# Seven-product rounds of a gated feed-forward: a chunk loaded in halves, copies moved behind product copies, one plain chunk more

## The reference

```python
mod = c_act @ w_ada[l] + b_ada[l]          # 6 x 1024 columns; the second block has 3 x 1024 more
...
h2 = rmsnorm(x, g_ffn[l]) * (1.0 + sc2) + sh2
gate, up = jnp.split(h2 @ w_gu[l], 2, axis=-1)      # D_FF = 2816 columns each
x = x + ga2 * ((jax.nn.silu(gate) * up) @ w_down[l])
```

## Time and profile before

| what | value |
|---|---|
| median of the runs (lowest, highest) | 1082.65 us (1078.78, 1084.9) |
| the profiled execution | 1086.33 us |
| its span in the profile | 1084.3 us |
| PE busy with matmuls | 1030.2 us, 95% |
| DVE, POOL, ACT busy | 755.5, 513.4 and 503.8 us |

### The profile page before, as it was taken

How to read it: one execution, slowest core, us unless ns; L and a number is a source line. 1 busy time by engine, 2 the same in 40 slices (tenths; PEclk the granted TensorE clock), 3 DMA queues, 4 the chain that set the end, 5 groups by cost and what they waited for, 6 DMA issues and landing times.

```text
span 1084.3 us, 15812 instructions
## 1 busy us (share of the span) xinstructions
PE 1030.2 (95%) x5814; PEld 862.4 (80%) x5814; DVE 755.5 (70%) x1423; ACT 503.8 (46%) x773; POOL 513.4 (47%) x209
## 2 busy tenths in 40 slices
PE   6999999999996898899989999999999999999997
PEld 5787796678885898899978788888887777888886
DVE  5367997787767344445549884579999999977322
ACT  4244335882454444544473223253445788363142
POOL 0034353681368544455543334345873767634350
PEclk9999999999999999989999999999999999999999
DMA  9984231141222223222239892323323222322312
GB/s 326 349 270 128 75 105 39 40 157 40 78 78 76 77 87 109 77 77 78 78 104 297 281 297 72 114 78 118 114 89 106 78 78 78 117 79 78 116 39 77
DMA packets 127257, 128.98 MB, mean 119 GB/s; under 512 B 3553, under 2 KB 125281, under 8 KB 127201
## 3 DMA queue, kind: packets, MB, share of 16 engines
q1 hardware_dynamic: 125952, 127.38, 36.4%
q10 hardware_dynamic: 1248, 0.86, 0.3%
HBM read 126.13 MB, written 2.10 MB: 118 GB/s over the span
## 4 chain that ended last, share of the span: by engine, by line
PE 69%; issue 12%; POOL 9%; DVE 4%; ACT 3%; DMA 2%; SPq 1%; POOLq 0%; DVEq 0%; ACTq 0%
PE bank L817 15%; PE bank L819 14%; PE bank L818 14%; POOL w_a L750 2%; POOL w_lo L653 2%; PE bank L1164 2%; PE bank L1135 2%; POOL w_hi L750 2%; PE bank L1007 2%; POOL w_s L757 2%; PE bank L1447 1%; PE bank L1449 1%; PE bank L1448 1%; DVE ff_lo L2534 1%; DMA ada_stage<-in_w_ada 1%
## 5 line engine op out<-in xcount | busy, mean ns | idle before, releaser
L653 POOL TENSOR_TENSOR w_lo<-w_stage,w_hi 128x2048 fp32r<-128x2048 f32 x59 | 283.2, 4801 | 376.9 <-ACT w_hi L1520 376.9
L817 PE MATMUL bank<-act_hi,w_hi 128*128 128x512 f32 x544 | 216.6, 398 | 3.5 <-POOL w_lo L653 3.5
L819 PE MATMUL bank<-act_hi,w_lo 128*128 128x512 f32 x544 | 212.1, 390 | 0.0
L818 PE MATMUL bank<-act_lo,w_hi 128*128 128x512 f32 x544 | 212.0, 390 | 0.0
L1520 ACT ACTIVATE w_hi<-w_stage 128x2048 fp32r<-128x2048 f32 x60 | 114.8, 1914 | 145.5 <-PE bank L819 133.0
L2698 DVE SCALAR_TENSOR_TENSOR bank<-v_pad,vcol,bank 128x512 f32<-128x512 f32 x208 | 138.2, 748 | 0.0
L817 PEld LDWEIGHTS bank<-act_hi,w_hi 128*128 128x128 f32 x544 | 102.2, 188 | 30.8 <-POOL w_lo L653 5.5
L818 PEld LDWEIGHTS bank<-act_lo,w_hi 128*128 128x128 f32 x544 | 102.3, 188 | 21.9 <-issue 1.4
L819 PEld LDWEIGHTS bank<-act_hi,w_lo 128*128 128x128 f32 x544 | 102.1, 188 | 21.5
L817 PE MATMUL bank<-ff_hi,w_hi 128*128 128x512 f32 x176 | 72.0, 409 | 3.5 <-POOL w_lo L653 3.5
L750 POOL TENSOR_TENSOR w_a<-w_stage,w_a 128x1024 fp32r<-128x1024 f32 x18 | 43.6, 2445 | 61.4 <-ACT w_a L1794 61.4
(11 more groups left out here) (404 smaller groups left out, 2610.1 us busy)
## 6 DMA issues: line engine op xcount, KB each, us to landing
w_stage<-in_w_in SPq DMA_DIRECT2D x29, 1024.0 KB, 5.2
w_stage<-in_w_gu SPq DMA_DIRECT2D x22, 1024.0 KB, 5.1
ada_stage<-in_w_ada SPq DMA_DIRECT2D x20, 1024.0 KB, 11.4
w_stage<-in_w_out SPq DMA_DIRECT2D x12, 1024.0 KB, 5.2
late_stage<-in_mod_w SPq DMA_DIRECT2D x12, 1024.0 KB, 8.4
w_stage<-in_w_down SPq DMA_DIRECT2D x8, 1024.0 KB, 5.3
late_stage<-in_w_ada SPq DMA_DIRECT2D x4, 1024.0 KB, 10.9
w_stage<-in_pw_w SPq DMA_DIRECT2D x4, 1024.0 KB, 5.4
```

Of the source, the lines that this page charges most:

```text
L653: nc.gpsimd.tensor_tensor(w_lo[b][:], w_stage[b][:], w_hi[b][:].bitcast(F32), ALU.subtract).then_inc(s_lo, 1)
L817: pe.matmul(dst, wh, rhs_hi(k), start=(first and k == 0), stop=False)
L818: pe.matmul(dst, wh, rhs_lo(k), start=False, stop=False)
L819: mm = pe.matmul(dst, wl, rhs_hi(k), start=False, stop=(last and k == n_k - 1))
```

## The change

- `PLAIN` is 3: three pairs of chunks are plain and eight are rounds. So there is one pair of 96 matmuls with 512 columns more and one round of 168 with 256 columns less.
- In the rounds the up chunk is loaded in two halves with a semaphore for the low one (`s_half`): the low half as soon as it has been copied and `w_diff` made, ahead of the gate chunk in SP's queue; the high half where the whole chunk was loaded. `copy_up_low` and `w_diff` wait for the low half, `weight_sum(0, 0)` and `block_hi(w_a22)` for the high one.
- In the round on ACT, `copy_block(p2_half[1])` stands ahead of `copy_up_low`, and `low_silu(1)` ahead of the second `gate_hi`.
- Ahead of the rounds the sums `h_sum` are made by DVE, no longer by POOL, and at once after the first plain chunk; the parts of `t_1`, `t_3`, `t_2` come ahead of the weight blocks.
- In the last round product 5 comes after products 6 and 7, and the parts of `ff` and of the first down chunk are made earlier.
- The late modulation columns: 6, 4, 6 between the steps for 5, 6, 5, and their loads and sums one place or two later.
- The last gained tile of the second block signals on another semaphore that was already there.

```diff
-PLAIN = 2
+PLAIN = 3
...
-LATE_BETWEEN = {0: 5, 2: 6, 4: 5}
+LATE_BETWEEN = {0: 6, 2: 4, 4: 6}
...
+            def low_half_free(r):
+
+                sp.wait_ge(s_diff, r + (DIFF0 + 1))
+                sp.wait_ge(s_sv, 2 * r + 2)
+
             def gate_stage_free(r):
 
                 sp.wait_ge(s_sadd, r * PER_SUM + SUM0)
-                sp.wait_ge(s_diff, r + (DIFF0 + 1))
-
-            def up_stage_free(r):
+
+            def high_half_free(r):
 
                 sp.wait_ge(s_blo, r * PER_PART + PART0)
 
             for r in range(ROUNDS - 1):
+                gate, up = [w_cols(a["w_gu"], 0, KD, c0 + (r + PLAIN + 1) * NCOL) for c0 in (0, D_FF)]
+                low_half_free(r)
+                sp.dma_start(w_stage[b_up][:, low_k, :], up[:, low_k, :]).then_inc(s_half, 16)
                 gate_stage_free(r)
...
+                sp.dma_start(w_stage[b_gate][:], gate).then_inc(s_stage[b_gate], 16)
+                high_half_free(r)
+                sp.dma_start(w_stage[b_up][:, high_k, :], up[:, high_k, :]).then_inc(s_stage[b_up], 16)
...
+                if not last:
+                    seventh()
                 pe.wait_ge(s_slo, r * PER_SUM + 2)
...
                 product(bank_a[1], w_s2, 1, b_t2, False)
+                if last:
+                    seventh()
...
-                    act.wait_ge(s_prod, ALL_PRODUCTS - (5, 1)[n - C_DOWN])
+                    act.wait_ge(s_prod, ALL_PRODUCTS - (6, 1)[n - C_DOWN])
...
                 copy_block(u2_half[0], BLOCK_BANK[0][0], at + (PROD0 + 2))
+                copy_block(p2_half[1], SHARED_BANK, at + (PROD0 + 3))
                 if not last:
                     copy_up_low(r + 1, 0)
                     copy_up_low(r + 1, 1)
-                copy_block(p2_half[1], SHARED_BANK, at + (PROD0 + 3))
...
+                    gate_hi(r + 1, 0)
+                else:
+                    ff_high(0, 4)
+                low_silu(1, made + (CV0 + 1))
+                act.wait_ge(s_prod, at + (PROD0 + 4))
...
             plain_out(0, 0)
             plain_out(0, 1)
+            for ks in (low_k, high_k):
+                V.tensor_tensor(h_sum[:, ks, :], act_hi[:, ks, :].bitcast(F32), act_lo[:, ks, :].bitcast(F32), ALU.add).then_inc(s_diff, 1)
...
                 out_low_left(1, at + (PROD0 + 4), r * PER_COPY + (COPY0 + 3))
-                out_high_right(0, at + (PROD0 + 5))
+                if last:
+                    ff_low(0, 4, 1)
+                out_high_right(0, at + (PROD0 + (7 if last else 5)))
```

More of the change, by code:

```diff
@@ L1295, in first_products @@
             def first_products(r):
-                pe.wait_ge(s_blo, r * PER_PART + (PART0 - 3) if not isinstance(r, int) or r else 1)
+                pe.wait_ge(s_blo, r * PER_PART + (PART0 - 3) if not isinstance(r, int) or r else 4)
                 if not isinstance(r, int):
@@ L1300, in first_products @@
                 product(bank_c, w_a12, 0, b_21, True)
-                pe.wait_ge(s_blo, r * PER_PART + (PART0 - 2) if not isinstance(r, int) or r else 2)
+                pe.wait_ge(s_blo, r * PER_PART + (PART0 - 2) if not isinstance(r, int) or r else 5)
                 if not isinstance(r, int):
@@ L1867, in act_round @@
                 else:
-                    for q in range(2):
-                        nc.scalar.activation(ff_hi[:, 4 * q:4 * q + 4, :], ff[:, 4 * q:4 * q + 4, :], ACT.Copy).then_inc(s_ffhi, 1)
+                    hi_part(C_DOWN, C_DOWN % 2, stage_uses(C_DOWN))
                 high_silu(0, made + (CV0 + 4))
@@ L2577, in dve_round @@
                     weight_sum_lo(0, 1, hi_at + 2)
-                else:
-                    ff_low(0, 4, 1)
                 out_low_right(0, at + (PROD0 + 9))
@@ L2583, in dve_round @@
                     weight_sum(1, 1, lo_at + 2)
-                right_product(t, 0, silu + (SG0 + 2))
-                out_high_right(1, at + (PROD0 + 10))
-                if not last:
+                    right_product(t, 0, silu + (SG0 + 2))
+                    out_high_right(1, at + (PROD0 + 10))
                     weight_sum_lo(1, 0, hi_at + 3)
@@ L2590, in dve_round @@
                     weight_sum(2, 1, lo_at + 4)
-                else:
-                    ff_low(4, 8, 2)
-                left_product(t + 1, 1, at + (PROD0 + (11 if last else 13)), silu + (SG0 + 1))
-                if not last:
-                    out_low_left(0, at + (PROD0 + 12), r * PER_COPY + (COPY0 + 6))
-                out_low_right(1, at + (PROD0 + (12 if last else 14)))
-                if not last:
-                    weight_sum_lo(2, 0, hi_at + 5)
-                right_product(t + 1, 1, silu + (SG0 + (3 if last else 4)))
-                if not last:
-                    weight_sum_lo(2, 1, hi_at + 6)
+                    left_product(t + 1, 1, at + (PROD0 + 13), silu + (SG0 + 1))
+                    out_low_left(0, at + (PROD0 + 12), r * PER_COPY + (COPY0 + 6))
+                    out_low_right(1, at + (PROD0 + 14))
+                    weight_sum_lo(2, 0, hi_at + 5)
+                    right_product(t + 1, 1, silu + (SG0 + 4))
+                    weight_sum_lo(2, 1, hi_at + 6)
+                else:
+                    right_product(t, 0, silu + (SG0 + 2))
+                    out_high_right(1, at + (PROD0 + 10))
+                    left_product(t + 1, 1, at + (PROD0 + 11), silu + (SG0 + 1))
+                    out_low_right(1, at + (PROD0 + 12))
+                    right_product(t + 1, 1, silu + (SG0 + 3))
             with dve.Fori(0, ROUNDS - 1) as r:
```

131 lines of the change are left out of this document (66 added, 65 removed).

## The result

The changed kernel takes 1047.16 us (median of 4, 1045.92 to 1049.44); the kernel before, on the same chip, 1083.66 us. The ratio is 0.9674, with a 95% interval of 0.9638 to 0.9709: faster, by 36.5 us. The forecast was 1036.5 with a range of 1029 to 1051, so the time lies within it, 10.7 us above the number. The main course alone had a range of 1030 to 1042, and 1047.16 is above that. The profiled execution took 1046.57 us, its span is 1044.7.

The account below looks back on a forecast made before the run. PE, busy for 95% of the span, was taken to set the time. Terms 12.0 - 51.2 - 4.6 - 3.9 = -47.7, less 1.5 given back, make -46.2: 1036.5 us on the median, range 1029 to 1051.

Parts of the forecast that it names:

- The main course: Whole kernel: the predicted course without any rival, chance 0.68, with its own range of 1030 to 1042 us.
- The bound and the rounds: PE sets the time; in the rounds its wait ahead of product 7 goes, giving 19.7 us a round for 23.64.
- The term of -51.2: From product 2 of the first round to that of the last: seven rounds, 137.9 us, for 189.15 before.
- the rival with 11.9: Slower or the same, chance 0.06: the up chunk's high half lands as slowly as 11.9 us, a round takes 28.
- The way in: From the second plain pair to product 2 of the first round: 50.1 us for 38.1, +12.0.
- The last round and the start of the down projection: From product 2 of the last round to the third pass: 40.2 us for 44.8, -4.6, bounds -6 and -1.
- The modulation columns: PE's 2.36 us wait for the fourth column goes, as it asks 5.5 us later; with 1.5 of clock, -3.9.
- Nothing later in the profile makes PE wait, so it keeps the gain to the end: Behind the modulation columns: no further wait of PE, so no term for the rest of the kernel.
- The clock: 1.5 us given back for a clock that falls once behind one of the new short waits.
- a longer way in: Rival, chance 0.15: the chain ahead of the first round takes longer, costing 4 to 8 us, about 1043.
- a wait in the rounds: Rival, chance 0.09: a new wait of 1 to 2 us and its clock in each of seven rounds, 1047 to 1062.
- sign of being wrong: Wait ahead of product 7, 12 or 13 each round, half landing after over 7 us, or PE idle over 3 before product 2.

Follow-up runs that it names:

- e4: Kernel before, with only ACT's copy of p2_half[1] put ahead of the two up stage copies in each round, up chunk still whole: 1060.48 us.
- e5: e1 with the up chunk of the rounds loaded whole again, the copies keeping their new order: 1045.83 us.
- e6: e1 with two plain pairs and the old order on POOL, ACT and DVE ahead of the rounds: 1041.79 us.
- e11: e1 with the two sums of normed values of 2048 elements back on POOL instead of DVE: 1037.93 us.
- e7: e1 with the last round, and the high parts behind it, as before the change on PE, ACT and DVE: 1041.68 us.
- e1: Changed kernel with ACT's high part of the fifth down chunk moved ahead of the square of tile 0: 1036.89 us.
- e2: Changed kernel with five late modulation columns instead of six ahead of residual 0, and five instead of four in the next stretch: 1048.10 us.
- e10: Kernel before, with the new tables of the modulation columns alone (loads, six columns ahead of residual 0, PE's sums later): 1089.65 us.
- e12: Changed kernel with five late columns ahead of residual 0 and PE's sums of columns 2 and 3 one tile pass sooner: 1045.10 us.
- e3: Changed kernel with the tables of the modulation columns (loads, order, sums on PE) as before the change: 1043.22 us.

## Why the prediction was right in the time and wrong in one step

- *The bound and the rounds*: right. The eight waits were ACT's order and the clock behind them. The term of -51.2 measured -52.6, since a round takes 19.51 and not 19.65 to 19.7 us. Which edit does it was not in the forecast: the order gives 3.2 us a round (e4), the halves 0.9, and once in the first round 4.5 and the slow clock behind it (e5). The half lands in 3.5 us; the rival with 11.9 is out.
- *The way in*: +12.3 for +12.0. I had 0.5 to 1 us of wait between the plain chunks and 1.5 ahead of product 2; the trace has none and 2.37. The last low part of the plain chunks ends 32.5 us after the start of the second plain pair (347.83 and 315.33), for 33.8 in the forecast, so PE need not wait for it. The size of the part has a check in e6: three plain pairs with the new order beat two with the old by 4.9 us in the medians and 4.5 to 6.3 in the rows. Moving the sums to DVE, which I had counted as removing 3.5 us, shortens the way in by 3.4 to 3.7 us in the rows (e11).
- *The last round and the start of the down projection*: -5.3 for -4.6; by e7 4.8 in the medians and 4.2 in the rows. The two short waits measured 0.61 and 0.52 (expected 0.9 and 0.8); the down projection started 18.4 us after product 1 of the last round, for 18.5.
- *The modulation columns*: this is the step that failed. Its stretch measured +7.8 for -3.9, and e1, which takes its wait away, is 10.3 us faster. "Now it asks for columns 2 and 3 one tile of 24 matmuls and more (5.5 us) later" was taken as pure gain: PE asks later, so it need not wait. (It is even two tiles, 11 us: they stand at 562.08, and the old place is behind the pass that ends at 551.) But PE does not only ask there, it also makes the sums from which DVE gets the gains of residual 0. Placed directly ahead of the fifth down chunk, whose high part stands behind the square of that residual on ACT, they close a loop of 8.7 us that PE must wait out (8.72 in e2 and in e10). The sixth column adds the last 1.0 to make 9.72; taking away both gives 5.83 (e12), the high part moved ahead of the square gives none (e1). Without this wait the kernel takes 1036.9 us, 0.4 from the number forecast, and its last stretch then measures -3.6 (491.5 us from 544.0 on) for the -3.9 of the forecast. The part is not alone in it: 5.83 us stay in e12, because PE comes to the fifth chunk 18.2 us after DVE's first late column in the changed kernel (563.0 and 544.87), where it took 25.8 before (615.34 and 589.54). Of these 7.6 us 4.0 are the wait and the slow clock that the new tables took away, and 2.7 come from DVE, whose first column ends 3.0 us after the start of the third tile pass and not 0.3.
- *"Nothing later in the profile makes PE wait, so it keeps the gain to the end"* was read from an absence. In the kernel before, PE wanted the fifth chunk at 615.3 and its low part had ended at 613.7, with PE just 2.4 us and a slow pass late. It was close, and no row of waits shows what is close. The two rows of before that do:

```profile
609.09 4.63 POOL L653 TENSOR_TENSOR w_lo<-w_stage,w_hi 128x2048 fp32r<-128x2048 f32 x1 [13.00 <-ACT w_hi L1520]
...
615.34 0.48 PE L817 MATMUL bank<-ff_hi,w_hi 128*128 128x512 f32 x1
```

- *The clock*: 1.5 us given back for one fall. From the plain chunks on it fell once, behind the new wait and not behind a short one: the 24 matmuls from 572.75 took 7.1 us, the next 24 5.6. In the rounds the window 366 to 502 has 1.00 for 0.94 before. There the clock had fallen behind seven of the eight waits, and a round lost 4.1 us with 2.4 of wait. The trace agrees with the rule that the prediction cites from the Trainium skill, "TensorE: Matmul & The Clock Gate", section "HAM oscillation — how this bites in real kernels", that gaps in PE's work bring the clock down again each time round a loop.
- *The miss of 10.7 us and luck*: between the two profiled executions it is 6.5 us (1046.57 for 1040.1), that is about the 11.7 of the last stretch less 1.8 of a start that no edit touched, less 1.8 of the other stretches together and less the 1.5 given back. The rest of the 10.7 is the choice of execution: the profiled one of before was 3.7 us above its median, that of the changed kernel 0.6 below. And that the time is within the range is in part luck. It lies above the main course's own 1030 to 1042; what covers it is the room made for a longer way in and a wait in the rounds, of which neither came. No rival and no sign of being wrong named a wait in the down projection.

What stays open: the two kernels start the plain chunks 1.8 us apart, with the same program up to there, and the times of e12 and of its profiled execution differ by 1.8 us. So of terms below 2 us only the rows speak, not the times, and rows are of one execution each. In how many executions of e1 or e11 the clock fell behind product 2 is not shown.

## What to carry to other kernels

Before a step of the critical engine is moved later because its input is late, ask who waits for its output; here the way led over DVE, ACT and POOL back to the very next thing that PE needed, 8.7 us long. And when a wait is removed, list for each thing that is needed afterwards by how much it was early: a slack that stood behind a stall is no slack. Last, a short instruction that somebody waits for belongs ahead of a long one that waits for a load: of 4.1 us lost in each round, 3.2 came back by moving one copy of 0.36 us.

## What the runs showed of the hardware

The same wait did and did not bring the clock down. In the changed kernel PE waits 2.37 us ahead of product 2, in e7 2.36 us at the same place. The four microseconds behind it, first in the changed kernel, then in e7 (columns as above, clock third from the end):

```profile
366.00:370.00 4.00, 4.00 (x36) 4.00 (x36) 0.00 (x0) 2.97 (x7) 4.00 (x3) 1.00 0.17 54
```
```profile
366.00:370.00 4.00, 3.87 (x20) 3.88 (x21) 0.07 (x1) 2.02 (x4) 4.00 (x3) 0.58 0.28 98
```

One goes on at 2.4 GHz, the other mostly at 1.2, and issues 20 matmuls for 36; product 7 then starts 7.0 us after product 2 in the one and 8.5 in the other. Seven kernels have this wait in the same place: in four (the changed kernel, e3, e5, e12) product 7 comes 7.0 us after product 2, in three (e1, e2, e7) 8.4 to 8.5, with nothing in between, behind waits of 2.36 to 2.71 and of 2.30 to 2.73 us. So the length of the wait alone does not say which. A wait of 1.87 us brought the clock down in e4 and e7 and not in the kernel before and in e10, and one of 3.4 us did in e4, e6, e10 and e11 and not in the kernel before. After waits of 0.2 to 0.9 us, from the plain chunks on, it did not fall in any of these kernels. So a wait of 2.3 to 2.7 us ahead of product 2 has a price with two values, 0 and 1.5 us, and single executions of two nearly equal kernels can differ by it.

A fall can also be free. In e7 the clock falls behind the 1.87 us wait ahead of product 13, and PE then waits 2.29 us at the start of the down projection; in e10 it stays, and PE waits longer (the rows of e7 stand above; here those of e10, and the three microseconds behind the first wait, e10 and then e7):

```profile
555.51 0.39 PE L1290 MATMUL bank<-act_hi,w_lo 128*128 128x256 f32 x1 [1.87 <-DVE tmp L2510]
...
562.11 0.80 PE L817 MATMUL bank<-ff_hi,w_hi 128*128 128x512 f32 x1 [3.49 <-POOL w_lo L653]
```
```profile
555.51:558.51 3.00, 3.00 (x24) 2.91 (x24) 2.48 (x2) 3.00 (x3) 1.95 (x1) 1.00 0.01 3
```
```profile
518.77:521.77 3.00, 3.00 (x19) 3.00 (x20) 2.48 (x2) 3.00 (x3) 1.95 (x1) 0.75 0.00 0
```

From the one wait to the end of the next are 6.6 us in both. The old way in shows the same: 16.9 us from the end of the 3.4 us wait to the rounds in the kernel before, without a fall and with a second wait of 5.7 us, and in e4, e6 and e10, with a fall and a second wait of 3.0, 4.1 and 2.8. Where another engine sets the end of the next wait, slow matmuls in front of it cost nothing more.

The other is that DVE's sums with two operands in SBUF were slow while POOL worked: four of 1024 elements took 4.74 us with POOL idle and, in e11, 13.47 us, where they began beside the last of POOL's sums (9.22 us for two) and went on beside its next low part. The shortest of these four took 1.21 us, the longest 5.61. The Trainium skill, "Advanced Engine Details and Errata", section "GPSIMD Details", says that POOL shares a read and a write interface with DVE and conflicts with DVE instructions that have two inputs in SBUF. The rows agree, with 8.7 us for four instructions.
